# Half the columns of each level in the two blocked inverses of block two

## The reference

```python
L = jnp.where(strict, jnp.einsum('bhnid,bhnjd->bhnij', k_beta, k) * gamma, 0.0)
eye = jnp.eye(C, dtype=L.dtype)
rhs = jnp.concatenate([v_beta, k_beta * jnp.exp(g)[..., None]], axis=-1)
sol = lax.linalg.triangular_solve(L + eye, rhs, left_side=True, lower=True, unit_diagonal=True)
```

## Time and profile before

| | |
|---|---|
| median of 3 runs | 2831.44 us (2831.38 to 2835.01) |
| span of the profiled execution | 2828.2 us |
| median of the runs less that span | 3.2 us |
| PE busy | 2802.1 us, 99% of the span |
| DVE busy | 1605.0 us, 57% |
| ACT busy | 1204.4 us, 43% |
| POOL busy | 86.0 us, 3% |

### The profile page before, as it was taken

How to read it: one execution, slowest core, us unless ns; L and a number is a source line. 1 busy time by engine, 2 the same in 40 slices (tenths; PEclk the granted TensorE clock), 3 DMA queues, 4 the chain that set the end, 5 groups by cost and what they waited for, 6 DMA issues and landing times.

```text
span 2828.2 us, 38622 instructions
## 1 busy us (share of the span) xinstructions
PE 2802.1 (99%) x16578; PEld 2370.2 (84%) x16578; DVE 1605.0 (57%) x1366; ACT 1204.4 (43%) x1066; POOL 86.0 (3%) x138
## 2 busy tenths in 40 slices
PE   8999999999999999999999999999999999999998
PEld 7888888888888888888888888998888888888887
DVE  6668554454555554554446688967664454544445
ACT  4465443333443343333335455544443333433333
POOL 0100000000000000002002000030000000000000
PEclk9999999999999999999999999999999999999999
DMA  7555555556555555555556645400455555555554
GB/s 240 172 169 189 164 175 190 188 191 194 190 182 192 193 184 188 191 188 187 193 194 203 198 159 178 149 3 33 150 186 189 188 192 188 185 192 192 193 193 165
DMA packets 257709, 501.57 MB, mean 177 GB/s; under 512 B 12406, under 2 KB 17857, under 8 KB 257201
## 3 DMA queue, kind: packets, MB, share of 16 engines
q1 hardware_dynamic: 257585, 499.72, 54.2%
HBM read 497.13 MB, written 2.10 MB: 177 GB/s over the span
## 4 chain that ended last, share of the span: by engine, by line
PE 95%; DVE 3%; ACT 1%; issue 0%; DMA 0%; SPq 0%; ACTq 0%; DVEq 0%
PE psum L762 24%; PE psum L764 24%; PE psum L763 24%; PE psum L748 9%; PE psum L747 5%; PE psum L1221 2%; DVE weight_lo L2046 1%; PE psum L813 1%; ACT weight_hi L1536 1%; PE psum L728 1%; PE psum L731 1%; PE psum L730 1%; PE psum L682 0%; PE psum L942 0%; PE psum L952 0%
## 5 line engine op out<-in xcount | busy, mean ns | idle before, releaser
L2046 DVE TENSOR_TENSOR weight_lo<-weight_raw,weight_hi 128x2048 fp32r<-128x2048 f32 x460 | 1054.3, 2292 | 1046.5 <-ACT weight_hi L1536 1044.6
L1536 ACT ACTIVATE weight_hi<-weight_raw 128x2048 fp32r<-128x2048 f32 x460 | 881.5, 1916 | 1371.1 <-PE psum L764 1199.3
L762 PE MATMUL psum<-weight_hi,h_both 128*128 128x512 f32 x1856 | 725.0, 391 | 0.9 <-DVE weight_lo L2046 0.9
L764 PE MATMUL psum<-weight_hi,h_both 128*128 128x512 f32 x1856 | 722.5, 389 | 0.0
L763 PE MATMUL psum<-weight_lo,h_both 128*128 128x512 f32 x1856 | 722.1, 389 | 0.0
L748 PE MATMUL psum<-h_both,weight_hi 128*128 128x512 f32 x1280 | 446.9, 393 | 0.0
L762 PEld LDWEIGHTS psum<-weight_hi,h_both 128*128 128x128 f32 x1856 | 348.5, 188 | 72.6 <-DVE weight_lo L2046 1.4
L764 PEld LDWEIGHTS psum<-weight_hi,h_both 128*128 128x128 f32 x1856 | 348.4, 188 | 72.7
L763 PEld LDWEIGHTS psum<-weight_lo,h_both 128*128 128x128 f32 x1856 | 348.5, 188 | 71.3
L747 PE MATMUL psum<-h_both,weight_lo 128*128 128x256 f32 x1280 | 361.2, 282 | 4.8 <-DVE weight_lo L2046 3.6
L748 PEld LDWEIGHTS psum<-h_both,weight_hi 128*128 128x128 f32 x1280 | 239.7, 187 | 53.4
(11 more groups left out here) (534 smaller groups left out, 2226.3 us busy)
## 6 DMA issues: line engine op xcount, KB each, us to landing
weight_raw<-in_w_in SPq DMA_DIRECT2D x144, 1024.0 KB, 5.4
weight_raw<-in_w_ffn_in SPq DMA_DIRECT2D x88, 1024.0 KB, 5.0
weight_raw<-in_w_ffn_out SPq DMA_DIRECT2D x44, 1024.0 KB, 5.0
weight_raw<-in_ffn_w_gate SPq DMA_DIRECT2D x44, 1024.0 KB, 5.1
weight_raw<-in_ffn_w_up SPq DMA_DIRECT2D x44, 1024.0 KB, 5.1
weight_raw<-in_ffn_w_down SPq DMA_DIRECT2D x44, 1024.0 KB, 5.0
weight_raw<-in_w_out SPq DMA_DIRECT2D x32, 1024.0 KB, 5.0
weight_raw<-in_w_branch_rnn SPq DMA_DIRECT2D x8, 1024.0 KB, 5.0
```

Source lines behind the costliest of these rows:

```text
L762: mm(acc[:, t, :], xh[:, c], wh[:, k, :], start=(start and k == 0), stop=False, skip_group_check=True)
L764: last = mm(acc[:, t, :], xl[:, c], wh[:, k, :], start=False, stop=(stop and k == CK - 1), skip_group_check=True)
L1536: A(hi[j % g.hi][:], raw[j % g.ring][:], ACT.Copy).then_inc(hi_ready, 1)
L2046: V.tensor_tensor(lo[r][:], raw[r][:], hi[j % g.hi][:].bitcast(F32), ALU.subtract).then_inc(lo_ready, 1)
```

## The change

A level changes only the left block column of each pair, 32 of the 64 columns. Before, all 64 are streamed, masked and added. After, PE streams the 32 (`left(x, k)` picks runs of b columns, one of each pair), its result lies packed in 32 columns per unit, and DVE masks and adds 256 elements per partition in place of 512. Z is kept packed in columns 0 to 31 of its slot. At level 4 Z is the stationary operand of the product that goes to xt, so its other 32 columns must be zero: POOL clears them once for each inverse, and PE waits for that. The stationary operands stay 64 columns wide everywhere, and transposes stay 64x64.

```diff
+        def left(x, k):
+            return x.rearrange("p (n m b) -> p n m b", m=2, b=2 ** (k + 1))[:, :, 0, :]
+
+        def lefts(x, k):
+            return x.rearrange("p u (n m b) -> p u n m b", m=2, b=2 ** (k + 1))[:, :, :, 0, :]
+
+        def packed(x, k, n):
+            return x.rearrange("p (u n b) -> p u n b", u=n, b=2 ** (k + 1))
...
+            gp.memset(z_r[:, :, 32:64], 0.0).then_inc(step("z_cleared"), 1)
+            gp.wait_ge(*at_step("z_cleared"))
             gp.wait_ge(*at_step("k_gram3"))
             gp.memset(state[:], 0.0).then_inc(S("rw_state"), 1)
...
             gp.wait_ge(S("gd_gam_masked"), 4)
+            gp.wait_ge(S("inv_z"), 20)
+            gp.memset(z_gc[:, :, 32:64], 0.0).then_inc(step("gd_z_cleared"), 1)
+            gp.wait_ge(*at_step("gd_z_cleared"))
             gp.wait_ge(S("rw_y_mm"), 4)
...
+            def of_left(o, lhs, rhs, n, k):
+                for u, c, r in halves(n):
+                    last = mm(o[r, u * 32:(u + 1) * 32].rearrange("p (n b) -> p n b", b=2 ** (k + 1)), lhs(r, u), rhs(r, u),
+                              start=(u == 0), stop=True, skip_group_check=True)
+                return last
...
-                of_chunks(bank(b % 2), lambda r, u: nt_r[r, u, :], lambda r, u: x_r[r, u, :], 8, 8 * b).then_inc(S("inv_z"), 1)
+                of_left(bank(b % 2), lambda r, u: nt_r[r, 8 * b + u, :], lambda r, u: left(x_r[r, 8 * b + u, :], k), 8,
+                        k).then_inc(S("inv_z"), 1)
...
-                x_lhs, x_rhs = (xt_r, z_r) if k < 4 else (z_r, xt_r)
-                of_chunks(bank(4 + b), lambda r, u: x_lhs[r, u, :], lambda r, u: x_rhs[r, u, :], 8, 8 * b).then_inc(S("inv_x"), 1)
+                if k < 4:
+                    of_left(bank(4 + b), lambda r, u: xt_r[r, 8 * b + u, :], lambda r, u: left(z_r[r, 8 * b + u, :], 4), 8,
+                            4).then_inc(S("inv_x"), 1)
+                else:
+                    pe.wait_ge(*at_step("z_cleared"))
+                    of_left(bank(4 + b), lambda r, u: z_r[r, 8 * b + u, :], lambda r, u: xt_r[r, 8 * b + u, 32:64].unsqueeze(1), 8,
+                            4).then_inc(S("inv_x"), 1)
...
-                V.tensor_tensor(z_r[:, u, :], bank(b % 2).rearrange("p (u n) -> p u n", u=8), bcc(low_c[k + 1], 8),
+                V.tensor_tensor(z_r[:, u, 0:32].rearrange("p u (n b) -> p u n b", b=2 ** (k + 1)), packed(bank(b % 2)[:, 0:256], k, 8),
+                                left(low_c[k + 1], k).unsqueeze(1).to_broadcast([P, 8, 16 >> k, 2 ** (k + 1)]),
                                 ALU.mult).then_inc(S("inv_z_out"), 1)
...
-                m = (x_r if k < 4 else xt_r)[:, u, :]
-                V.tensor_tensor(m, m, bank(4 + b).rearrange("p (u n) -> p u n", u=8), ALU.add).then_inc(S("inv_x_out"), 1)
+                if k < 4:
+                    m = lefts(x_r[:, u, :], k)
+                    V.tensor_tensor(m, m, packed(bank(4 + b)[:, 0:256], k, 8), ALU.add).then_inc(S("inv_x_out"), 1)
+                else:
+                    m = xt_r[:, u, 32:64]
+                    V.tensor_tensor(m, m, bank(4 + b)[:, 0:256].rearrange("p (u n) -> p u n", u=8), ALU.add).then_inc(S("inv_x_out"), 1)
```

More of the change, by code:

```diff
@@ L287, in build @@
         STEPS = {
-            "gpsimd": ["rows_cleared", "means_made", "masks_built", "pair_built", "reset_built", "centre_made", "rw_fm", "eyes_made", "akt_masked0", "akt_masked1", "rkt_masked0", "rkt_masked1"],
+            "gpsimd": ["rows_cleared", "means_made", "masks_built", "pair_built", "reset_built", "centre_made", "rw_fm", "eyes_made", "akt_masked0", "akt_masked1", "rkt_masked0", "rkt_masked1", "z_cleared", "gd_z_cleared"],
             "tensor": ["f_total", "lora_mm", "lora_turned", "rates0", "rates1", "g_mm", "gd_tok", "kk_sum", "kk_bc", "rk_sum", "gd_l2", "l2_bc", "k_gram0", "k_gram1", "k_gram2", "k_gram3",
@@ L1359, in chunk_z @@
                 pe.wait_ge(S("gd_x_out"), 2 * k + b + 1)
-                of_chunks(bank(b), lambda r, u: nt_g[r, u, r], lambda r, u: x_gc[r, u, :], 8, 8 * b).then_inc(S("gd_z"), 1)
+                of_left(bank(b), lambda r, u: nt_g[r, 8 * b + u, r], lambda r, u: left(x_gc[r, 8 * b + u, :], k), 8,
+                        k).then_inc(S("gd_z"), 1)
             def chunk_x(k, b):
@@ L1364, in chunk_x @@
                 pe.wait_ge(S("gd_xt_out"), 2 * k + b + 1)
-                last = of_chunks(bank(4 + 2 * b), lambda r, u: xt_gc[r, u, :], lambda r, u: z_gc[r, u, :], 8, 8 * b)
+                last = of_left(bank(4 + 2 * b), lambda r, u: xt_gc[r, 8 * b + u, :], lambda r, u: left(z_gc[r, 8 * b + u, :], 4), 8, 4)
                 if k == 4:
-                    last = of_chunks(bank(b), lambda r, u: z_gc[r, u, :], lambda r, u: xt_gc[r, u, :], 8, 8 * b)
+                    pe.wait_ge(*at_step("gd_z_cleared"))
+                    last = of_left(bank(b), lambda r, u: z_gc[r, 8 * b + u, :], lambda r, u: xt_gc[r, 8 * b + u, 32:64].unsqueeze(1), 8, 4)
                 last.then_inc(S("gd_x"), 1)
@@ L2808, in chunk_z @@
                 dve.wait_ge(S("gd_z"), 2 * k + b + 1)
-                V.tensor_tensor(z_gc[:, u, :], bank(b).rearrange("p (u n) -> p u n", u=8), bcc(low_c[k + 1], 8),
+                V.tensor_tensor(z_gc[:, u, 0:32].rearrange("p u (n b) -> p u n b", b=2 ** (k + 1)), packed(bank(b)[:, 0:256], k, 8),
+                                left(low_c[k + 1], k).unsqueeze(1).to_broadcast([P, 8, 16 >> k, 2 ** (k + 1)]),
                                 ALU.mult).then_inc(S("gd_z_out"), 1)
@@ L2814, in chunk_x @@
                 dve.wait_ge(S("gd_x"), 2 * k + b + 1)
-                for o, x in ((4 + 2 * b, x_gc), (b, xt_gc))[:2 if k == 4 else 1]:
-                    V.tensor_tensor(x[:, u, :], x[:, u, :], bank(o).rearrange("p (u n) -> p u n", u=8),
-                                    ALU.add).then_inc(S("gd_x_out" if x is x_gc else "gd_xt_out"), 1)
+                m = lefts(x_gc[:, u, :], k)
+                V.tensor_tensor(m, m, packed(bank(4 + 2 * b)[:, 0:256], k, 8), ALU.add).then_inc(S("gd_x_out"), 1)
+                if k == 4:
+                    m = xt_gc[:, u, 32:64]
+                    V.tensor_tensor(m, m, bank(b)[:, 0:256].rearrange("p (u n) -> p u n", u=8), ALU.add).then_inc(S("gd_xt_out"), 1)
             def query_gram(c):
```

## The result

The changed kernel takes 2861.27 us, the median of 4 runs (2860.01 to 2868.88), against 2831.62 (2831.38 to 2835.01) for the kernel before: ratio 1.0109, interval 1.0097 to 1.0121. It is slower by 30 us, where 2828.5 had been forecast. The profiled execution has a span of 2858.3 us and took 2860.01, 1.7 us more; so in the 3.2 us that the forecast added to the span of before, about 1.5 is how far the median of the runs lay above the profiled one, an estimate.

A forecast was written before the change was run, and what follows sets the result against it. PE, busy for 99% of the span, was taken as the bound, in the gated delta inverse in turn with DVE. Span 2828.2 less six terms of 2.9 us is 2825.3; with 3.2 for the median, 2828.5; range 2822 to 2832.

The forecast's parts named there:

- PE's pace: Both inverses: weight load sets PE's pace, so batches stay at 0.93 us and PE's own work saves nothing.
- DVE's price: 62 edited DVE instructions in both inverses fall from about 0.68 to 0.42 us each, 16 us of DVE's time.
- The six terms: Shorter PE waits for DVE in both inverses and behind them, 2.9 us in sum.
- terms 1 to 3: RWKV inverse: level 0 gains 0.2 us, levels 1 to 4 gain 0.2, PE's waits behind the inverse 0.6.
- term 4: Gated delta inverse, levels 1 and 2: four edited instructions shorten the DVE chain that PE awaits, 1.0 us.
- term 5: Gated delta inverse, levels 3 and 4: PE's 0.53 us wait for z(0) shrinks, 0.5 us gained.
- term 6: End of the gated delta inverse: the last two adds, ahead of the values, get shorter, 0.4 us.
- The sign for term 4: In the gated delta inverse PE's wait of 1.36 us should fall to about 0.3.
- POOL: Clearings of 1.0 and 0.5 us on POOL, and PE's waits for them, cost nothing.
- the third rival: Clock falls in the inverses as the stream halves; 20 us of RWKV work at the lower level gives 2848.5; chance 0.05.
- The rival in which the stream sets the pace: Inverse batches fall towards 0.47 us and DVE takes over; gain 16 us, 2815; chance 0.08.
- the one in which DVE's gain isn't there: Strided DVE instructions save nothing or later waits absorb the gain; time as before, 2831.4 us; chance 0.14.

The follow-up runs named there:

- e8: Changed kernel with the stationary operand of inverse products at levels 1 to 4 (bar gated delta's xt product) cut to 32 columns, values incomplete; 2823.21 us.
- e9: e1_twice with the stationary operand of inverse products at levels 1 to 4 (bar gated delta's xt product) cut to 32 columns, values incomplete; 2826.86 us.
- e1_twice: Changed kernel with each narrow product streaming its 32 columns twice, the second copy into an unread half of the PSUM bank; 2827.67 us, ratio 0.9983.
- e2: e1_twice with the products of the RWKV inverse alone streaming their 32 columns once; 2847.66 us, ratio 1.0059.
- e3: e1_twice with the products of the gated delta inverse alone streaming their 32 columns once; 2844.57 us, ratio 1.0042.
- e5_dve_only: Kernel before with PE's products untouched; DVE adds only left blocks and masks only them, except z at levels 0 and 4; 2828.57 us, ratio 0.9991.
- e4_z_narrow: e1_twice with only the z products of both inverses streaming their 32 columns once; 2832.13 us, one run.
- e7_x_narrow: e1_twice with only the x products of both inverses streaming their 32 columns once; 2832.13 us, one run.
- e10_filler: Changed kernel with one 128x128 identity product, its result unread, added ahead of each of the 62 batches; 2903.09 us, one run.

## Why the prediction was wrong, point by point

**PE's pace: right.** "I take the pace of a batch as unchanged, 0.93 us": 0.93 and 0.94 at full clock, and e8 and e9 show that it is the weight load that held it there. What was off is the sign by which it was to be seen: the record's duration did not fall by 27 ns. Line 1241 (duration in ns, min/median/max) in the kernel after, first over both clock levels, then at full clock alone:

```profile
L1241 PE MATMUL psum<-rw_x,rw_gram x640: 189/219/313, 1860.7 to 1926.8; 64*64 64x32 f32 x160
...
L1241 PE MATMUL psum<-rw_xt,rw_z x128: 219/219/219, 1923.1 to 1928.7; 64*64 64x32 f32 x128
```

At full clock it is 219, and the median of before was 218. The start-to-start time is the thing to read, not the duration.

**DVE's price: right.** 0.42 us was taken, 0.42 is measured in every group (410 to 422 ns), against 0.68, and the edited instructions save 16 us together. DVE's busy time as a whole fell by 14.2.

**The six terms: near in sum, once the clock holds.** They can't be read in the kernel after, whose clock fell, but they can in e1_twice, which has DVE's side whole. PE, order of time, the kernel before and then e1_twice:

```profile
1861.06 1.10 PE L1200 MATMUL psum<-a_tilde_r,proj 64*64 64x128 f32 x32 [0.27 <-ACT rw_gram L1882]
...
1919.71 1.08 PE L1317 MATMUL psum<-rwkv_state,rw_wt 64*64 64x64 f32 x29
```

```profile
1862.34 1.10 PE L1214 MATMUL psum<-a_tilde_r,proj 64*64 64x128 f32 x32 [0.27 <-ACT rw_gram L1917]
...
1919.37 1.08 PE L1350 MATMUL psum<-rwkv_state,rw_wt 64*64 64x64 f32 x29
...
1964.05 2.08 PE L1244 MATMUL psum<-gd_x_chunks,gd_nt 64*64 64x64 f32 x64 [1.01 <-DVE gd_x_chunks L2857]
...
1971.59 1.15 PE L1244 MATMUL psum<-gd_z_chunks,gd_xt_chunks 64*64 64x64 f32 x32
...
1980.08 3.81 PE L1490 MATMUL psum<-gd_v_beta,gd_xt 128*128 128x128 f32 x32 [0.75 <-DVE gd_xt L2911]
```

The RWKV inverse takes 57.03 us instead of 58.65: terms 1 to 3 bring 1.6 where 1.0 was given. From its end on, e1_twice is ahead by 0.34 us; at the products of level 3 by 1.40 (1964.05 against 1965.45), so term 4 is 1.06 (given 1.0); at level 4 by 1.94 (1971.59 against 1973.53), term 5 is 0.54 (0.5), and its wait is gone; at the values by 2.31 (1980.08 against 1982.39), term 6 is 0.37 (0.4). Sum 3.6 against 2.9. (In this pair of traces e1_twice began the inverse 1.28 us later, so 2.3 of the 3.6 are left at the values, and the spans differ by the same 2.3.) The sign for term 4 was wrong: the wait of 1.36 fell to 1.01 and not to 0.3, because an earlier one for the same chain (one of the two waits for line 2809) went first. A chain's gain is spread over all the waits along it.

**POOL: right.** 0.94 us for the first clearing and 0.52 for the second; the state was ready at 1878.4 (1877.7 had been forecast, in a stage that now began 1.0 us later), and nobody waited.

**The clock: the step that failed.** The step stood in the third rival: "Against: PE is not idle for longer than before anywhere". It took idle time as what counts, gave the case 0.05, and left the clock out of the sum as a term of nothing. The facts in the same paragraph were right, a tile's stream on for 27 of 58 ns instead of 54, and they were the thing to weigh: the pace was held by the load, so the whole cut in columns had to come out of the array's activity. e1_twice gives the columns back at the same pace and the clock stays; e2 and e3 put the fall in the inverse that is narrow. The term that was missing measures 33.6 us (kernel after against e1_twice). The rival's price for one inverse was about right: it took 20 us of PE's work at the lower level as 20 us lost, and e2_rwkv_narrow loses 20.0 against e1_twice. It left out the second inverse, 16.9 more in e3_gd_narrow. In the kernel after the clock came back only with denser products (lines 1315 and 1483). The Trainium skill, "TensorE: Matmul & The Clock Gate", section "Why this matters for your kernels", names gaps in which PE is idle as what costs the clock in the middle of a kernel; by that the clock of this kernel should have held. Here the trace disagrees, with PE busy for 10.00 of 10.00 us in the stretch ahead of the fall.

The rival in which the stream sets the pace is refuted (0.93). So is the one in which DVE's gain isn't there, by e1_twice; e5_dve_only points the same way, though its interval reaches 1.0.

**The better version** is e1_twice: 0.9983 (0.9974 to 0.9992) of the kernel before, the one version here whose interval lies below 1. It streams as many columns as the kernel before, at the same pace of 0.93 us, and keeps DVE's gain. The change on PE itself buys nothing in it: e5_dve_only, which leaves PE alone, has 0.9991 (0.9982 to 1.0), and the two aren't told apart.

## What to carry to other kernels

Where the weight load sets PE's pace, fewer streamed columns save no time, and they can cost: compare for how much of the time a tile's stream is on, before and after, and if that drops, give the clock a term of its own in the sum. PE "busy" in a profile does not say that its array is. This is one kernel, with float32 products of 64x64 tiles; how far the share may drop before the clock falls isn't shown. If the clock falls, try a duplicated stream inside the loads' shadow first, and read the granted clock of the stretch before any chain of waits.

## What the runs showed of the hardware

- The granted clock fell to 0.50 with PE busy for all of 37.5 and 41.0 us, and held at 1.00 in e8_short_load between 1890 and 1900 us with PE busy for 7.40 of 10.00.
- The load is slower at the lower level as well, so a pace that it sets suffers too: 0.93 to 1.71 us per batch of 32 records.
- Where narrow and full batches took turns (e4_z_narrow, e7_x_narrow), and where both load and stream were short (e8_short_load), the clock fell for pieces of 3.4 to 6.8 us and came back inside the inverse, 10.2 to 13.6 us in all.
- Load and stream overlap, and the longer sets the pace of a batch: 0.93 (64 weight columns, 32 streamed), 0.90 (32, 64), some 0.52 (32, 32).
- A 128x128 float32 product between batches of 64x64 tiles costs 0.54 us at full clock and 0.86 at the lower level (e10_filler), and did not keep the clock up.
